# Attention of the second block: its score, turn and value steps set between the four projections and the two halves of the output product, and the softmax sums divided out behind the value product

## The reference, cut to what matters

```python
q = (h @ w_q).reshape(...); k = hn @ w_k; v = hn @ w_v
s = einsum(q, k) * HEAD_DIM ** -0.5 + relative_bias      # per head
s = where(valid, s, NEG_INF)
p = softmax(s, axis=-1)
o = einsum(p, v).reshape(bsz, seq, D_MODEL)
m = o @ w_o
h = h + rms_norm_2(m, g[1])
f = sq_relu_mlp(rms_norm_2(h, g[2]), w_up, w_down)
```

## Time and profile before

| | |
|---|---|
| median of 3 runs | 1899.41 us (1896.49 to 1901.89) |
| the profiled execution's own time | 1900.48 us |
| its span, first to last instruction | 1898.7 us |
| mean granted TensorE clock | 0.872 of full |
| busy shares: PE, DVE, ACT | 79%, 32%, 24% |

### The profile page before, as it was taken

One profiled execution on the slowest core, in us unless ns is written; L12 is line 12 of the kernel. 1 busy time (PEld: TensorE's weight loads), 2 busy tenths in 40 slices (PEclk: granted clock), 3 DMA queues, 4 the chain that ended last, 5 costly groups with the idle time before them and its releaser, 6 DMA issues.

```text
span 1898.7 us, 20794 instructions
## 1 busy us (share of the span) xinstructions
PE 1492.6 (79%) x8793; PEld 945.2 (50%) x8793; DVE 611.6 (32%) x770; ACT 455.8 (24%) x641; POOL 97.8 (5%) x88
## 2 busy tenths in 40 slices
PE   3968799877777667766667666759999999789998
PEld 2966577422222112222122221217789978778887
DVE  3475755300000000000000000016655555765553
ACT  3442452200000000000000000024644444454442
POOL 2453200000000000000000000000000000000000
PEclk8988899887877888778887788779999999999999
DMA  9522487899999999999999999995444546324440
GB/s 344 159 89 89 178 285 301 332 427 427 430 428 429 429 427 430 426 430 429 428 429 427 430 427 429 429 390 199 144 178 179 191 152 207 131 96 178 178 178 22
DMA packets 97875, 565.29 MB, mean 298 GB/s; under 512 B 4780, under 2 KB 6072, under 8 KB 73240
## 3 DMA queue, kind: packets, MB, share of 16 engines
q1 hardware_dynamic: 95080, 555.81, 72.5%
q0 software_dynamic: 2112, 7.06, 1.2%
q10 hardware_dynamic: 624, 1.57, 0.2%
HBM read 563.37 MB, written 1.05 MB: 297 GB/s over the span
## 4 chain that ended last, share of the span: by engine, by line
PE 43%; DMA 43%; DVE 8%; ACT 4%; issue 2%; POOL 0%; SPq 0%; DVEq 0%; ACTq 0%; POOLq 0%
DMA ring_b<-in_w_exp_down_dram 19%; DMA ring_b<-in_w_exp_up_dram 19%; PE PS L1921 11%; PE PS L1922 10%; PE PS L1923 10%; PE PS L2226 3%; PE PS L2250 2%; DVE parts L1193 1%; DMA ring_a<-in_a_w_in_dram 1%; PE PS L1904 1%; DMA ring_a<-in_w_exp_up_dram 1%; DMA ring_a<-in_ada_w_dram 1%; ACT parts L753 1%; PE PS L2054 1%; DVE arena L1310 1%
## 5 line engine op out<-in xcount | busy, mean ns | idle before, releaser
L1193 DVE TENSOR_TENSOR parts<-ring_a,parts 128x2048 fp32r<-128x2048 f32 (+1 forms) x101 | 231.1, 2292 | 174.5 <-ACT parts L753 174.1
L2226 PE MATMUL PS<-ring_a,arena 128*32 128x512 f32 x1232 | 175.1, 698 | 107.8 <-DMA ring_a<-in_w_exp_up_dram 65.7
L753 ACT ACTIVATE parts<-ring_a 128x2048 fp32r<-128x2048 f32 (+1 forms) x101 | 191.6, 1901 | 188.1 <-PE PS L1923 188.0
L2226 PE MATMUL PS<-ring_b,arena 128*32 128x512 f32 x768 | 129.8, 810 | 99.8 <-DMA ring_b<-in_w_exp_up_dram 63.8
L1604 DVE TENSOR_TENSOR arena<-PS,arena 128x512 f32<-128x512 f32 x16 | 11.1, 691 | 562.9 <-PE PS L2226 562.9
L2226 PEld LDWEIGHTS PS<-ring_a,arena 128*32 128x32 f32 x1232 | 35.9, 118 | 240.3 <-DMA ring_a<-in_w_exp_up_dram 104.9
L976 ACT ACTIVATE arena<-PS 128x512 f32<-128x512 f32 x16 | 9.6, 597 | 565.2 <-PE PS L2226 565.2
L1921 PE MATMUL PS<-parts,hT 128*128 128x512 f32 (+1 forms) x352 | 130.9, 372 | 12.0 <-DVE parts L1193 6.9
L1921 PE MATMUL PS<-hT,parts 128*128 128x256 f32 x448 | 128.2, 286 | 9.8 <-POOL hT L636 9.8
L2250 PE MATMUL PS<-ring_b,arena 128*32 128x512 f32 x720 | 102.5, 703 | 42.0 <-DMA ring_b<-in_w_exp_down_dram 41.9
L1922 PE MATMUL PS<-parts,hT 128*128 128x512 f32 (+1 forms) x352 | 128.1, 364 | 0.0
(11 more groups left out here) (315 smaller groups left out, 2157.8 us busy)
## 6 DMA issues: line engine op xcount, KB each, us to landing
ring_a<-in_w_exp_gate_dram SPq DMA_DIRECT2D x45, 2048.0 KB, 25.6
ring_b<-in_w_exp_down_dram SPq DMA_DIRECT2D x45, 2048.0 KB, 26.2
ring_a<-in_w_exp_up_dram SPq DMA_DIRECT2D x32, 2048.0 KB, 25.6
ring_b<-in_w_exp_up_dram SPq DMA_DIRECT2D x32, 2048.0 KB, 26.4
ring_a<-in_w_exp_down_dram SPq DMA_DIRECT2D x16, 2048.0 KB, 27.1
ring_b<-in_w_exp_gate_dram SPq DMA_DIRECT2D x16, 2048.0 KB, 23.5
ring_a<-in_w_up_dram SPq DMA_DIRECT2D x16, 2048.0 KB, 7.8
ring_a<-in_w_down_dram SPq DMA_DIRECT2D x16, 2048.0 KB, 7.6
```

The lines of the kernel that those rows point to most:

```text
L753: act.activation(part_of(c, 0), raw(c), ACT.Copy).then_inc(chunk_high, 1)
L1193: dve.tensor_tensor(part_of(c, 1), raw(c), part_of(c, 0).bitcast(F32), ALU.subtract)\
L2226: ins = mm(PS[32 * j:32 * j + 32, side, :], xe[:, 2 * q + kk, :], w[:, kk, j * NB:(j + 1) * NB], start=q == 0 and kk == 0, stop=q == 3 and ...
```

## The change

- Order of the projections, of their slabs and chunks: `bk0`, `bq0`, `bk1`, `bq1`. PE scores groups 0 and 2 between the halves of `bk1`, turns group 0 and scores group 3 ahead of `bq1`, and turns group 2 between the halves of `bq1`. Groups go in the order 0, 2, 3, 1, 4, 5.
- The probabilities are not multiplied by the inverted sums. PE turns them as ACT leaves them. DVE inverts the sums (`invert`), and PE spreads them over 64 rows with matmuls against the identity, the sum as a stationary operand repeated 64 times, behind the value matmuls (`b_values`). ACT copies these rows to SBUF (`sum_rows`), DVE multiplies the attended values by them (`scale_out`), ACT takes the high and DVE the low part (`attended`). Groups 2 and 3, and 4 and 5, share one job: four jobs `bo0`, `bo23`, `bo1`, `bo45` in place of six.
- Of `bT3`, `bT1` and `bT4` ACT copies both halves.
- The score and value matmuls alternate between the two halves of rows or columns of the array.
- The output product goes by half (`bm_half`): heads 0 to 7 of tile 0 after `bo0`, with group 5's scores inside it, then the rest of tile 0, then tile 1. Its chunks are split in that order.
- ACT runs a one-element root after the last exponential. Several buffers move.

```diff
-    + [("nT4t0", 2, 2), ("bvr1", 2, 0), ("nT4t1", 2, 3), ("bvr0", 2, 1), ("bk0", 2, 0), ("bk1", 2, 1), ("bq0", 2, 2), ("bq1", 2, 3)]
-    + [("bs0", 2, 1), ("bs1", 2, 2), ("bs2", 2, 3), ("bT0", 2, 0), ("bs3", 2, 1), ("bo0", 1, 2), ("bT1", 2, 3), ("bs4", 2, 0)]
-    + [("bo1", 1, 1), ("bT2", 2, 2), ("bs5", 2, 3), ("bo2", 1, 0), ("bT3", 2, 1), ("bo3", 1, 2), ("bT4", 2, 3), ("bo4", 1, 0)]
-    + [("bT5", 2, 1), ("bo5", 1, 2), ("bmt0", 2, 0), ("bmt1", 2, 1), ("nT5t0", 2, 2), ("nT5t1", 2, 0), ("up10", 2, 0), ("up11", 2, 2)]
+    + [("nT4t0", 2, 2), ("bvr1", 2, 0), ("nT4t1", 2, 3), ("bvr0", 2, 1), ("bk0", 2, 0), ("bq0", 2, 1), ("bk1", 2, 2), ("bs0", 2, 3)]
+    + [("bs2", 2, 0), ("bT0", 2, 3), ("bs3", 2, 0), ("bq1", 2, 1), ("bT2", 2, 2), ("bo0", 1, 3), ("bT3", 2, 0), ("bs1", 2, 1)]
+    + [("bo23", 1, 2), ("bs4", 2, 0), ("bmt0", 2, 3), ("bs5", 2, 1), ("bT1", 2, 2), ("bT4", 2, 0), ("bo1", 1, 2), ("bo45", 1, 0)]
+    + [("bT5", 2, 1), ("bmt1", 2, 1), ("nT5t0", 2, 2), ("nT5t1", 2, 0), ("up10", 2, 0), ("up11", 2, 2)]
...
-B_SLABS = [(j, j) for j in ("bv0", "bv1", "bk0", "bk1", "bq0", "bq1", "bm0", "bm1")]
+B_SLABS = [(j, j) for j in ("bv0", "bv1", "bk0", "bq0", "bk1", "bq1", "bm0", "bm1")]
...
+CHUNKS[-3:-1] = CHUNKS[-2], CHUNKS[-3]
...
+B_POS = {n: i for i, n in enumerate((0, 2, 3, 1, 4, 5))}
+B_OUT = {"bo0": (0, 0), "bo23": (1, 0), "bo1": (0, 4), "bo45": (1, 4)}
...
-        bp = [at(kb, 1024) for kb in (16, 20, 24, 28)]
-        bqT = at(36, 2048).rearrange("p (k s) -> p k s", k=KD)
+        bp = [xn[:, 0, :], xn[:, 1, :], at(16, 1024), at(44, 1024)]
+        bqT = at(28, 2048).rearrange("p (k s) -> p k s", k=KD)
...
-        bpt = [at(32, 1024), at(44, 1024)]
+        bpt = [at(20, 1024), at(24, 1024)]
+        bout = at(36, NB)
+        brows = at(38, NB)
+        soft = crep.rearrange("p k m -> p (k m)")
...
+        def softmax_of(n):
+            units = 8 if n < 2 else 4
+            i = 8 * B_POS[n]
+            pr = bp[B_POS[n] % 4].rearrange("p (u w) -> p u w", u=units)
+            return units, pr, soft[:, i:i + units], soft[:, 48 + i:48 + i + units]
+        def out_and_sums(job):
+            v = banks(job)
+            return (v[:, :, 0:S], v[:, :, S:NB]) if len(job) == 4 else (v[:, 0, :], v[:, 1, :])
+        def like_out(job, v):
+            return v.rearrange("p (j w) -> p j w", j=2) if len(job) == 4 else v
+        def out_blocks(job, i):
+            t, b0 = B_OUT[job]
+            return hT[i][:, b0:b0 + 4, t * P:(t + 1) * P]
...
-                        wait_drained(act, "bs5")
+                        wait_drained(act, "bs3")
...
-            for job, dst in (("bk0", bkT[:, 2:4]), ("bk1", bkT[:, 6:8]), ("bq0", bqT[:, 2:4]), ("bq1", bqT[:, 6:8])):
-                split_to(CHUNK_OF[job] + 3)
-                copy_out(job, dst.rearrange("p k s -> p (k s)"), 1)
...
             def b_softmax(n):
-                units = 8 if n < 2 else 4
-                pr = bp[n % 4].rearrange("p (u w) -> p u w", u=units)
-                act.wait_ge(row_max, 5 + n)
+                units, pr, maxima, sums = softmax_of(n)
+                act.wait_ge(row_max, 5 + B_POS[n])
                 for u in range(units):
-                    ins = act.activation(pr[:, u, :], pr[:, u, :], ACT.Exp,
...
                 ins.then_inc(row_exp, 1)
...
+            def b_turned(n, halves=(1,)):
+                for b in halves:
+                    copy_out(f"bT{n}", bpt[B_POS[n] % 2][:, b * NB:(b + 1) * NB], b)
+            def sum_rows(job):
+                wait_full(act, job)
+                act.activation(like_out(job, brows), out_and_sums(job)[1], ACT.Copy).then_inc(sum_rows_out, 1)
+            def attended(job):
+                wait_drained(act, job)
+                act.activation(out_blocks(job, 0), bout.rearrange("p (b s) -> p b s", b=4), ACT.Copy).then_inc(out_high, 1)
+            split_to(C_BK + 3)
+            product_out("bk0")
+            split_to(C_BK + 5)
+            product_out("bq0")
+            split_to(C_BK + 7)
             b_softmax(0)
+            b_softmax(2)
+            product_out("bk1")
+            b_turned(0)
+            split_to(C_BM)
+            b_softmax(3)
+            b_turned(2)
+            split_to(C_BM + 1)
+            product_out("bq1")
+            sum_rows("bo0")
+            b_turned(3, (0, 1))
+            attended("bo0")
+            split_to(C_BM + 2)
+            sum_rows("bo23")
             b_softmax(1)
-            for n in range(6):
-                b_turned(n)
-                if n < 4:
-                    b_softmax(n + 2)
+            attended("bo23")
+            b_softmax(4)
+            b_turned(1, (0, 1))
+            sum_rows("bo1")
+            b_turned(4, (0, 1))
             split_to(C_BM + 3)
+            attended("bo1")
+            b_softmax(5)
+            act.activation(std[:, 5, 0:1], std[:, 4, 0:1], ACT.Sqrt)
+            b_turned(5)
+            sum_rows("bo45")
+            attended("bo45")
...
-                dve.tensor_scalar(m, m, -1.0, None, ALU.mult).then_inc(row_max, 1)
-            def b_attended(n):
-                job = f"bo{n}"
-                wait_full(dve, job)
-                b0, per, cols = (4 * n, 4, slice(0, P)) if n < 2 else (2 * (n - 2), 2, slice(P, S))
-                src = bank(job, 0)[:, 0:per * P].rearrange("p (b s) -> p b s", b=per)
-                high, low = (hT[i][:, b0:b0 + per, cols] for i in range(2))
-                link(dve.tensor_copy(high, src))
-                dve.tensor_tensor(low, src, high.bitcast(F32), ALU.subtract).then_inc(psum_drained[pair(job)], 1)
-            def b_probs(n):
-                units = 8 if n < 2 else 4
-                dve.wait_ge(row_exp, n + 1)
-                normalise(4 + n, bp[n % 4].rearrange("p (u w) -> p u w", u=units), units)
+                link(dve.tensor_reduce(maxima, pr, AX, ALU.max))
...
+            def invert(n):
+                sums = softmax_of(n)[3]
+                dve.wait_ge(row_exp, B_POS[n] + 1)
+                dve.reciprocal(sums, sums).then_inc(sums_inverted, 1)
...
+            def scale_out(k, job):
+                dve.wait_ge(sum_rows_out, k + 1)
+                if k:
+                    dve.wait_ge(out_low, k)
+                dve.tensor_tensor(like_out(job, bout), out_and_sums(job)[0], like_out(job, brows), ALU.mult)\
+                    .then_inc(psum_drained[pair(job)], 1)
+            def attended(k, job):
+                dve.wait_ge(out_high, k + 1)
+                dve.tensor_tensor(out_blocks(job, 1), bout.rearrange("p (b s) -> p b s", b=4), out_blocks(job, 0).bitcast(F32),
+                                  ALU.subtract).then_inc(out_low, 1)
+            split_to(C_BK + 3)
+            product_out("bk0")
+            split_to(C_BK + 5)
+            product_out("bq0")
+            split_to(C_BK + 6)
             b_scores(0)
+            b_scores(2)
+            split_to(C_BK + 7)
+            product_out("bk1")
+            b_turned(0)
+            invert(0)
+            b_scores(3)
+            split_to(C_BM)
+            invert(2)
+            b_turned(2)
+            split_to(C_BM + 1)
+            invert(3)
+            product_out("bq1")
+            scale_out(0, "bo0")
             b_scores(1)
-            b_probs(0)
-            b_scores(2)
-            for n in range(6):
-                b_turned(n)
-                if n < 5:
-                    b_probs(n + 1)
-                if n < 3:
-                    b_scores(n + 3)
-                b_attended(n)
+            split_to(C_BM + 2)
+            attended(0, "bo0")
+            scale_out(1, "bo23")
+            b_scores(4)
+            invert(1)
+            attended(1, "bo23")
+            b_scores(5)
+            invert(4)
+            scale_out(2, "bo1")
+            attended(2, "bo1")
             split_to(C_BM + 3)
+            invert(5)
+            b_turned(5)
+            scale_out(3, "bo45")
+            attended(3, "bo45")
...
+            def turned(job, act, between=lambda: None):
...
+                        between()
...
-            for j in ("bk0", "bk1"):
-                turned(j, hR)
-            wait_drained(pe, "nT4t0")
-            wait_drained(pe, "nT4t1")
-            for j in ("bq0", "bq1"):
-                turned(j, hT)
...
+                for j in ("bk", "bq"):
+                    wait_drained(pe, f"{j}{b0 // 4}")
+                begin(job)
+                for i in range(per):
+                    for g in range(2):
+                        rows = slice(64 * g, 64 * g + 64)
                         ins = mm(bank(job, g)[:, i * w:(i + 1) * w], bqT[rows, b0 + i, t * P:(t + 1) * P],
                                  bkT[rows, b0 + i, k0:S], start=True, stop=True)
                 end(ins, job)
...
-                pe.wait_ge(prob_ready, 5 + n)
-                turn(f"bT{n}", [bp[n % 4][:, i * P:(i + 1) * P] for i in range(8)])
...
+                pe.wait_ge(row_exp, B_POS[n] + 1)
```

(79 more changed lines are left out.)

54 lines of the change are left out of this document (20 added, 34 removed).

## The result

| | median of runs, us | lowest to highest | profiled execution, own time | its span | mean granted clock |
|---|---|---|---|---|---|
| before | 1899.49 (6 runs) | 1896.49 to 1903.74 | 1900.48 | 1898.7 | 0.872 |
| after | 1890.35 (6 runs) | 1885.31 to 1891.86 | 1891.86 | 1890.1 | 0.874 |

The ratio is 0.9933, with a 95% interval of 0.9914 to 0.9952: the kernel became faster, by 9.1 us between the two medians (these alone stand at 0.9952, the upper end of the interval). The forecast was 1893.2, and its likeliest class was "within 0.3%".

A forecast was written before the change was run, and what follows sets the result against it. The attention stage was taken as bound by DVE's list, with PE waiting. Some twenty pieces put tile 0's squares 6.2 us earlier: 1900.48 - 6.2 = 1894.3, less 1.1 for a median, 1893.2; range 1889 to 1899.

The forecast's parts named there:

- 2: projections end: Scores 0, 2, 3 and turns 0, 2 between projections add 5.6 us of PE; projections end at 1639.9, not 1634.3.
- 3: `bmt0` starts: After the projections DVE leads through scores 1, a chunk's low part and `attended(0)`, to 1651.1; `bmt0` starts at 1651.5.
- 5: its second half starts: PE waits 1.9 us before group 4's values, then for ACT's and DVE's parts of `bo1`; second half at 1668.9.
- 6: squares of tile 0: First squares at 1680.0, behind `sum_rows` and `attended` of `bo45` in ACT's list; 4.3 us of readiness given away.
- 7: first matmul of the MLP: The old chain of 13.3 us follows the squares, 6.2 us earlier than before, and leads to 1693.3.
- Prices: Costs per piece of work: 0.09 us a score or value record, 1.5 us a group of 16 value records.
- alternating halves run side by side: Rival: alternating at each matmul halves the 0.09 us of some 130 records, 5.9 us more gain, 1887.3; chance 0.07.
- steps 5 and 6: Waits: PE 1.9 us for ACT's `bT4` copies behind `sum_rows("bo1")`; tile 0's squares behind group 5, 4.3 us.
- largely lost: Rival: falling clock or serial waits leave a gain of 2 to 5 us, 1894.5 to 1897.5; chance 0.20.
- priced for 1693: A second clock dip, at 1693, costing up to 1.5 us.
- Slower: Rival: clock gate takes small matmuls for idleness, output product runs at 1.2 GHz, 14.1 us more, 1907.3; chance 0.06.
- buy nothing by itself: Removing six normalisations of 1.22 us and copies' parts from DVE gains nothing alone, as PE leads in most steps.

The follow-up runs named there:

- e1: Changed kernel with score, value and sum matmuls one half after the other, not in turn: stage 103.0 us (101.8 after), median 1889.93 us.
- e10: Changed kernel with DVE's low part first, and value and sum matmuls not in turn: stage 100.5 us against 98.3, one run 1889.01 us.
- e11: Changed kernel with DVE's low part first, and score matmuls alone not in turn: stage 99.4 us against 98.3, one run 1888.18 us.
- e7: Changed kernel with ACT's copies of `bT4` ahead of `sum_rows("bo1")`, and its `attended("bo1")` ahead of the last split: stage 100.2 us, median 1885.29 us.
- e8: Changed kernel with e6's and e7's orders, and tile 0's squares, gain and residual ahead of group 5's last steps: stage 94.1 us, median 1883.74 us.
- e6: Changed kernel with DVE's split of a chunk moved behind `attended(0)`, the scaling of `bo23` and scores 4: stage 98.3 us, median 1886.61 us.
- e12: e6's kernel without ACT's one-element root: stage 98.34 us against 98.31, one run 1891.97 us.
- e4: Changed kernel with probabilities scaled by the inverted sums before the turns, without sum matmuls and `sum_rows`: stage 102.7 us, median 1889.46 us.
- r1: The changed kernel run again, unchanged: stage 101.8 us, median 1890.71 us.
- e5: Changed kernel with scores 0, 2, 3 and turns 0, 2 put back behind the four projections: stage 110.9 us, median 1900.86 us.
- e9: Changed kernel with the first half product kept in place and done again in a whole, late product: stage 110.4 us, median 1902.42 us.
- e2: Kernel before with only score and value matmuls alternating between halves: stage 111.4 us against 111.3, median 1900.48 us, ratio 1.0002.
- e3: Changed kernel with tile 0's output product in one piece behind all attended values: stage 112.8 us, median 1899.71 us.

## Why the prediction was right, and where it was not

The mechanism was right, and so was the order of events, by the prediction's own steps (from `bk0`, us):

| step | forecast | after | e1 |
|---|---|---|---|
| 2: projections end | 51.8 | 51.3 | 51.8 |
| 3: `bmt0` starts | 63.4 | 61.1 | 62.8 |
| 5: its second half starts | 80.8 | 78.4 | 79.1 |
| 6: squares of tile 0 | 91.9 | 88.5 | 89.7 |
| 7: first matmul of the MLP | 105.1 | 101.8 | 103.0 |

- **The step that failed is a price**, that of a score, value or sum record at 0.09 us (Prices, used in steps 2 to 6). Sixteen value or sum records took 0.9 to 1.0 us in a row of pieces, 0.06 each. The stage became 9.5 us shorter, not 6.2. Of the 3.3 between them, 2.1 are already in e1, whose order is the one that I had priced. The same price accounts for 1.3 of them: `bo0` and `bo1` with their sums took 2.5 for 3.0 each, group 5 with its sums 2.0 for 2.3 (what group 4 saved went into PE's wait behind it). The other 1.2 come from alternating halves, net.
- **The rival "alternating halves run side by side" was true in kind**, for all its chance of 0.07, and too large in size: 3.3 of the stage (e10, e11) rather than 5.9. I argued against it from four column groups in the first block. Those records move 512 columns, four times as many as a value record, so their 0.09 was no floor for two halves in turn. The Trainium skill's rule (TensorE: Matmul & The Clock Gate, The mechanism), that weight loads overlap running matmuls only where the row group differs, does not hold here: value records of both halves use all rows, and alternating the column half took them from 0.082 us, start to start (13 records in 1.25, e1), to 0.055. The Trainium skill (TensorEngine Tiling (Array Packing), Key Properties) says that different tiles load and multiply in parallel; the trace agrees, with this 0.055.
- **The waits** of steps 5 and 6 came as forecast, and e7 and e8 recover them. Step 3 had DVE lead through the split ahead of `attended(0)`, but with PE's own work ending 0.3 us before `bmt0`. With the faster records PE waited 1.24 (e1) and 1.86 us (after), and that split alone was worth the 1.9 (e6).
- **The clock** fell twice, as the rival "largely lost" had it. At `bmt0`, not at step 5's wait, it cost 1.6 us; the other, priced for 1693, came at the start of the MLP and cost nothing that shows. The faster records paid for the first one twice over. "Slower" did not happen: the product ran at 0.51 for 3.5 us and at the full level after.
- **Luck** has a part in how near 1893.2 came, 2.9 us off: the records were worth 4.6 more than priced (the 1.3 above, and 3.3), and the first fall with the longer wait ahead of it took back some 2.2 (1.6, and 1.86 - 1.24).
- **What was costed at nothing** was worth nothing: the early root (e12), and the DMAs (no idle time of PE, ACT or DVE in the stage is ended by one). Deferred normalisation was said to buy "nothing by itself"; e4 says 0.9.
- **The chances.** The border between faster and same stood half a microsecond above my value, with 0.38 of the forecast's chance below it and 0.24 above, and all of the rival "largely lost" above it. Every small piece had been priced with its tail, so these errors all went one way; a nearly even range around such a sum is the second mistake.

Open: why the clock fell behind an idle 1.86 us after, in e7, in r1 and, 0.9 us into the product, in e5, and did not in e9 behind the same 1.86; and why it fell in e2 behind the 1.28 that left it whole in before. Also open are the last 0.8 of e1's 2.1 us.

## What to carry to other kernels

Price a small matmul by the distance from one piece's start to the next's, never by a piece's length, which holds a tail; and where two tiles of the array can be fed in turn, try it, and then look at what the freed time turns into: here part went into longer waits for DVE, and part into a fall of the clock. When work is laid over another stage, undo each half of the move alone: here either of them held the whole gain, so they are one change. After such a move look again at what stands ahead of the new critical steps in the other engines' lists: three reorderings that compute the same brought 7.7 us of the stage, nearly as much as the 9.5 of the change, and 5.9 us between the medians.

## What the runs showed of the hardware

- Alternating the two 64-column halves at each matmul: 16 value records (128*64 by 128x128) take 1.09 us instead of 1.55 before. Scores by 128 columns, from the two halves of the rows in turn: 1.16 instead of 1.71 for 16. Scores by 256 columns: 1.13 in turn and 1.14 one half after the other (e1), no gain.
- Records of two halves mix even where the program does not alternate, if a piece of one half follows a piece of the other (e1).
- A stationary operand with step zero costs nothing extra: 16 sum records take 1.04 us, 16 value records 1.09.
- Behind an idle 1.85 or 1.86 us the granted clock fell to half in four of five executions (after: 0.51 for 3.5 us), and stayed whole in one (e9). Behind 1.28 us it fell in e2 (0.55 for 3.6 us) and not in before, and behind 2.3 us at the start of the MLP it fell in after and r1 and not in e1 and e6. So the length of the one idle time does not tell. Between small matmuls with a half product among them it was 1.00 over 30.6 us (e9), without it 0.76 over 32 (e3).
